# Inverting the recurrence's triangular blocks by 32x32 tiles of TensorE, with a last step that joins pairs

## The reference, cut to what matters

```python
def _rwkv7_step(S, inp):
    r, w, k, v, kk, b = inp
    sa = jnp.einsum('bhvk,bhk->bhv', S, kk)
    S = S * w[:, :, None, :] - sa[..., None] * b[:, :, None, :] + v[..., None] * k[:, :, None, :]
    return S, jnp.einsum('bhvk,bhk->bhv', S, r)
S_f, y_f = lax.scan(_rwkv7_step, S0_f, (r, decay[:, :, 0], kd[:, :, 0], v, kk, bd[:, :, 0]))
S_b, y_b = lax.scan(_rwkv7_step, S0_b, (r, decay[:, :, 1], kd[:, :, 1], v, kk, bd[:, :, 1]), reverse=True)
```

## Time and profile before

| | us |
|---|---|
| median of 3 runs | 4876.69 (4873.02 to 4878.9) |
| the profiled execution, first to last instruction | 4866.1 |
| TensorE matmuls busy | 4241.5 (87%) |
| DVE busy | 2749.5 (57%) |
| ACT busy | 1537.1 (32%) |
| POOL busy | 1475.8 (30%) |

### The profile page before, as it was taken

The page is one execution under the profiler, slowest core; times in us unless marked ns, Lnnn a source line. Parts: engine busy times, 40 slices in busy tenths (PEclk is TensorE's granted clock), DMA queues, the critical chain, the costliest instruction groups (busy, mean ns, idle before and its releaser), DMA issues. The chain is left out here.

```text
span 4866.1 us, 103654 instructions
## 1 busy us (share of the span) xinstructions
PE 4241.5 (87%) x43026; PEld 3280.6 (67%) x43026; DVE 2749.5 (57%) x4666; ACT 1537.1 (32%) x2721; POOL 1475.8 (30%) x1090
## 2 busy tenths in 40 slices
PE   6999889877998799989986998689788988978898
PEld 4887688854667587778884666578545677854566
DVE  3465444455666447544445665665575656557565
ACT  1332222223552123222222553210155421015542
POOL 2232233302013323233331111565232135523213
PEclk8999999988999899989998999789899999989999
DMA  6455532342135445642324133533403253340325
GB/s 194 146 186 189 145 78 59 81 159 83 42 83 178 148 153 198 197 122 71 78 59 148 45 92 112 172 99 106 149 7 81 67 183 124 104 142 17 81 53 181
DMA packets 517941, 561.41 MB, mean 115 GB/s; under 512 B 112732, under 2 KB 412284, under 8 KB 515380
## 3 DMA queue, kind: packets, MB, share of 16 engines
q1 hardware_dynamic: 389876, 475.93, 31.6%
q10 hardware_dynamic: 127616, 78.95, 5.6%
HBM read 366.75 MB, written 192.23 MB: 115 GB/s over the span
## 5 line engine op out<-in xcount | busy, mean ns | idle before, releaser
L1096 PE MATMUL pr_acc<-hH,pr_wh 128*128 128x512 f32 (+1 forms) x1288 | 482.4, 375 | 0.0
L1097 PE MATMUL pr_acc<-hL,pr_wh 128*128 128x512 f32 (+1 forms) x1288 | 466.0, 362 | 0.0
L1098 PE MATMUL pr_acc<-hH,pr_wl 128*128 128x512 f32 (+1 forms) x1288 | 465.6, 361 | 0.0
L2586 ACT ACTIVATE an_p<-an_p,an_stat 128x1280 f32<-128x1280 f32 (+5 forms) x372 | 339.7, 914 | 162.8 <-DVE an_stat L2664 157.2
L2033 POOL TENSOR_TENSOR rk_ml<-rk_lmask,rk_g 128x384 f32<-128x384 f32 x240 | 232.1, 999 | 464.1 <-DVE rk_g L1963 464.1
L2526 PE MATMUL an_t<-ident,an_p 128*128 128x128 f32 x2152 | 319.5, 283 | 40.3 <-ACT an_pT L2593 27.8
L2619 POOL TENSOR_TENSOR an_kl<-an_k,an_kh 128x1280 fp32r<-128x1280 f32 (+3 forms) x36 | 78.5, 2179 | 898.5 <-DVE an_qh L2644 898.5
L2526 PEld LDWEIGHTS an_t<-ident,an_p 128*128 128x128 f32 x2152 | 236.7, 142 | 163.9 <-issue 68.0
L2660 DVE CUSTOM_DVE_ANT_0 an_p<-an_s,an_mask 128x256 f32<-128x256 f32 (+8 forms) x308 | 274.9, 892 | 101.7 <-PE an_s L2509 68.4
L1971 DVE TENSOR_TENSOR rk_tu<-rk_tu,rk_ps 128x512 f32<-128x512 f32 x300 | 190.3, 634 | 237.0 <-PE rk_ps L1796 237.0
L1465 POOL TENSOR_TENSOR sp_sl<-sp_w,sp_sh 128x512 fp32r<-128x512 f32 x172 | 246.0, 1437 | 196.8 <-DVE sp_sh L1540 178.4
(11 more groups left out here) (382 smaller groups left out, 10181.1 us busy)
## 6 DMA issues: line engine op xcount, KB each, us to landing
CHK<-ri_out SPq DMA_DIRECT2D x24, 1920.0 KB, 8.1
rk_in<-CHK SPq DMA_DIRECT2D x120, 384.0 KB, 5.9
pr_w<-in_w_in ACTq DMA_DIRECT2D x58, 512.0 KB, 4.1
UT<-pr_out SPq DMA_DIRECT2D x45, 640.0 KB, 4.6
sp_w<-in_w_in ACTq DMA_DIRECT2D x50, 512.0 KB, 5.2
U<-sp_c SPq DMA_DIRECT2D x100, 256.0 KB, 2.0
mod_w<-in_w_mod SPq DMA_DIRECT2D x16, 1024.0 KB, 8.0
mo_w<-in_w_out SPq DMA_DIRECT2D x16, 1024.0 KB, 9.6
```

The costliest lines, as they stand in the source:

```text
L1096: nc.tensor.matmul(out, wh[:, u, k, 0:m], hi, start=(k == 0), stop=False)
L1097: nc.tensor.matmul(out, wh[:, u, k, 0:m], lo, start=False, stop=False)
L1098: ins = nc.tensor.matmul(out, wl[:, u, k, 0:m], hi, start=False, stop=(k == KT - 1))
L2586: nc.scalar.activation(row, row, ACT.Exp, bias=stat[:, n % NPM, j, 1:2], scale=heads[groups[n][0]].scale, accum_out=total[:, n % 4, j:j + ...
```

## The change

The five levels of 64x64 become four levels on diagonal pieces of 32x32 (`QB`) and a last step of another kind.

- Levels 1 to 4: each product is 32x32 with 32 columns, and four of them (one per 32 partitions, `quarter`) take the place of two. `TU`, `Ws` and `ML` hold 32 columns instead of 64, so the evictions by ACT and DVE and the masks by POOL are half as wide, and POOL makes `ML` for both heads in one instruction.
- Last step: `level_w` multiplies the piece that joins the two halves of a chunk with one half's inverse (two products of 32x32 per problem in the place of two of 64x64). `join` computes the correction and, with a product with minus the identity, moves the other half's inverse beside it. DVE writes both, negated, to a new tile `LU`. `join` of group 1 uses the banks of `state`, and waits for its evictions; group 0 of `outputs` waits for group 1 of the join's eviction instead.
- `solve` makes 32 of a chunk's 64 rows from `LU` (64 rows of the array) and 32 from `TU` (32 rows), two products in the place of one.
- `grams` writes the first piece of `G` as two halves of 32 columns (near, the diagonal quarters, and far, the ones between), with eight products each, and the rest by one product of 64 and one of 128 columns.
- One more constant, `eye`, is loaded, and the masks change with it.

```diff
                     for d in range(2):
-                        for j, arr in enumerate((A_BH, A_KH)):
+                        for far in range(2):
+                            for i in range(4):
+                                for h in range(2):
+                                    o = bank[h][quarter[i], d * 256 + far * QB:d * 256 + (far + 1) * QB]
+                                    nc.tensor.matmul(o, D[half[h], u, g, d, A_BH, quarter[i]], D[half[h], u, g, d, A_KT, quarter[i ^ far]],
+                                                     start=True, stop=True)
+                        for arr, a0, n, at0 in ((A_BH, A_RT, 1, CH), (A_KH, A_KT, 2, P)):
                             for c in range(2):
                                 for h in range(2):
-                                    rows, tok = half[h], half[c]
-                                    o = bank[h][half[c], d * 256 + j * P:d * 256 + (j + 1) * P]
-                                    ins = nc.tensor.matmul(o, D[rows, u, g, d, arr, tok], D[rows, u, g, d, A_KT:A_RT + 1, tok],
+                                    o = bank[h][half[c], d * 256 + at0:d * 256 + at0 + n * CH]
+                                    ins = nc.tensor.matmul(o, D[half[h], u, g, d, arr, half[c]], D[half[h], u, g, d, a0:a0 + n, half[c]],
                                                            start=True, stop=True)
...
                     for q in range(4):
-                        for c in range(2):
-                            ins = nc.tensor.matmul(wbank(u, g)[half[c], q * CH:(q + 1) * CH], TU[half[c], u, g, q, 1, :],
-                                                   pair[half[c], :], start=True, stop=True)
+                        for i in quarter:
+                            ins = nc.tensor.matmul(wbank(u, g)[i, q * QB:(q + 1) * QB], TU[i, u, g, q, 1, :], eye[i, 0, :],
+                                                   start=True, stop=True)
...
                         d, h = q // 2, q % 2
-                        for c in range(2):
-                            ins = nc.tensor.matmul(wbank(u, k)[half[c], q * CH:(q + 1) * CH], ML[half[c], u, g, d, h, lv, :],
-                                                   TU[half[c], u, g, q, 0, :], start=True, stop=True)
+                        if lv < NLEV - 1:
+                            for i in quarter:
+                                ins = nc.tensor.matmul(wbank(u, k)[i, q * QB:(q + 1) * QB], ML[i, u, g, d, h, lv, :],
+                                                       TU[i, u, g, q, 0, :], start=True, stop=True)
+                        else:
+                            for c in range(2):
+                                i, far = quarter[2 * c + d], quarter[2 * c + 1 - d]
+                                ins = nc.tensor.matmul(wbank(u, k)[far, h * QB:(h + 1) * QB], G[i, u, g, d, h, 0, QB:CH],
+                                                       TU[i, u, g, q, 0, :], start=True, stop=True)
...
-                    o = dbank(n).rearrange("p (q a k) -> p q a k", q=4, a=2)
+                    o = dbank(n)[:, 0:8 * QB].rearrange("p (q a k) -> p q a k", q=4, a=2)
                     for q in range(4):
-                        if lv < NLEV - 1:
+                        for i in quarter:
+                            nc.tensor.matmul(o[i, q, 0, :], TU[i, u, g, q, 1, :], Ws[i, g, q, :], start=True, stop=True)
+                        for i in quarter:
+                            ins = nc.tensor.matmul(o[i, q, 1, :], Ws[i, g, q, :], TU[i, u, g, q, 1, :], start=True, stop=True)
+                    ins.then_inc(pd.sem, 1)
+
+                def join(b, u, g):
+
+                    n = ND - NP + g
+                    pe.wait_ge(aw.sem, aw.nth(NW * b + NW - 2 * NP + g + 1))
+                    if g == 0:
+                        pe.wait_ge(dl.sem, dl.nth(ND * b + n))
+                    elif g == 1:
+                        pe.wait_ge(dh.sem, dh.nth(2 * b))
+                        pe.wait_ge(dy.sem, dy.nth(2 * b))
+                    else:
+                        pe.wait_ge(dl.sem, dl.nth(ND * b + n - 1))
+                    o = join_at(g)
+                    for h in range(2):
+                        for d in range(2):
                             for c in range(2):
-                                nc.tensor.matmul(o[half[c], q, 0, :], TU[half[c], u, g, q, 1, :], Ws[half[c], g, q, :],
-                                                 start=True, stop=True)
-                        for c in range(2):
-                            ins = nc.tensor.matmul(o[half[c], q, 1, :], Ws[half[c], g, q, :], TU[half[c], u, g, q, 1, :],
-                                                   start=True, stop=True)
+                                i, far = quarter[2 * c + d], quarter[2 * c + 1 - d]
+                                nc.tensor.matmul(o[i, d, h, :], Ws[far, g, h, :], TU[far, u, g, 2 * d + h, 1, :], start=True, stop=True)
+                                ins = nc.tensor.matmul(o[far, d, h, :], eye[far, 1, :], TU[far, u, g, 2 * d + h, 1, :],
+                                                       start=True, stop=True)
                     ins.then_inc(pd.sem, 1)
...
                     for q in range(4):
+                        d, h = q // 2, q % 2
                         for c in range(2):
-                            ins = nc.tensor.matmul(wbank(u, k)[half[c], q * P:(q + 1) * P], TU[half[c], u, g, q, 1, :],
-                                                   X[half[c], g, q, :], start=True, stop=True)
+                            near, far = quarter[2 * c + d], quarter[2 * c + 1 - d]
+                            nc.tensor.matmul(wbank(u, k)[far, q * P:(q + 1) * P], LU[half[c], g, d, h, :], X[half[c], g, q, :],
+                                             start=True, stop=True)
+                            ins = nc.tensor.matmul(wbank(u, k)[near, q * P:(q + 1) * P], TU[near, u, g, q, 1, :], X[near, g, q, :],
+                                                   start=True, stop=True)
                     ins.then_inc(pw.sem, 1)
...
-                        pe.wait_ge(dh.sem, dh.nth(2 * b))
-                        pe.wait_ge(dy.sem, dy.nth(2 * b))
+                        pe.wait_ge(dl.sem, dl.nth(ND * b + ND - 1))
                         pe.wait_ge(dbk.sem, dbk.nth(NP * b + NP))
...
-                    both = slice(0, 2) if lv < NLEV - 1 else slice(1, 2)
-                    o = TU[:, u, g, :, both, :]
-                    nc.vector.tensor_tensor(o, o, dbank(n).rearrange("p (q a k) -> p q a k", q=4, a=2)[:, :, both, :],
-                                            ALU.subtract).then_inc(dl.sem, 1)
+                    if lv < NLEV - 1:
+                        o = TU[:, u, g, :, :, :].rearrange("p q a k -> p (q a k)")
+                        nc.vector.tensor_tensor(o, o, dbank(n)[:, 0:8 * QB], ALU.subtract).then_inc(dl.sem, 1)
+                    else:
+                        nc.vector.tensor_scalar(LU[:, g], join_at(g), -1.0, None, ALU.mult).then_inc(dl.sem, 1)
...
                         for d in range(2):
-                            for h in range(2):
-                                ins = nc.gpsimd.tensor_tensor(ML[:, u, g, d, h, :, :], lm[:, d, :, :],
-                                                              G[:, u, g, d, h, 0:1, :].to_broadcast([P, NLEV, CH]), ALU.mult)
+                            ins = nc.gpsimd.tensor_tensor(ML[:, u, g, d], lm[:, d, :, :].unsqueeze(1).to_broadcast([P, 2, NLEV - 1, QB]),
+                                                          G[:, u, g, d, :, 0:1, 0:QB].to_broadcast([P, 2, NLEV - 1, QB]), ALU.mult)
```

More of the change, by code:

```diff
@@ L1597 @@
 NLEV = 6
+QB = CH // 2
 def rwkv_core(core):
@@ L1642, in rwkv_core @@
         half = [slice(0, CH), slice(CH, P)]
+        quarter = [slice(i * QB, (i + 1) * QB) for i in range(P // QB)]
         def wbank(u, k):
@@ L1648, in dbank, with join_at @@
             return bank[4 + (n + 1) % 2]
+        def join_at(g):
+            i = 6 if g == 1 else 4
+            return banks[:, i * 512:(i + 2) * 512].rearrange("p (d k) -> p d k", d=2)[:, :, 0:2 * QB].rearrange("p d (h k) -> p d h k", h=2)
         def qbank(g, c):
@@ L1882, in block_of @@
                         level_w(b, u, lv, 1)
-                        level_d(b, u, lv, 0)
-                        level_w(b, u, lv, 2)
-                        level_d(b, u, lv, 1)
-                        level_d(b, u, lv, 2)
+                        if lv < NLEV - 1:
+                            level_d(b, u, lv, 0)
+                            level_w(b, u, lv, 2)
+                            level_d(b, u, lv, 1)
+                            level_d(b, u, lv, 2)
+                        else:
+                            join(b, u, 0)
+                            level_w(b, u, lv, 2)
+                            join(b, u, 1)
+                            join(b, u, 2)
                         first = isinstance(b, int) and b == 0
@@ L3586, in constants @@
     f["mask_gram"] = np.zeros((2, P, 4 * CH))
```

(12 more changed lines are left out.)

22 lines of the change are left out of this document (14 added, 8 removed).

## The result

The changed kernel takes 5787.56 us (median of 4 runs, 5780.1 to 5793.56), the kernel before 4874.85 (4 runs, 4869.65 to 4878.9). The ratio is 1.187, 95% interval 1.185 to 1.189. The sign was forecast, the size was not: 5350 us was predicted, and 5787.56 lies above the range. About half of the +913 us has a cause that the prediction had priced at 1 us per block.

What follows compares the result with a forecast made beforehand. TensorE, fed by instruction pages, was taken as the bound: 67.0 (pages) + 1.5 (head) + 1.0 (solve) = 69.5 us per block against 45.9, times 20 is +472 us, about 5350 us, range 5210 to 5500.

Steps and rivals of the forecast that it cites:

- the solve: Solve's alternating 64-row and 32-row products: 1.0 us per block (0 to 6) beyond the time of their instruction pages.
- 100 ns or more: Sign in the solve: this start-to-start spacing would indicate the switches rival; 27 ns would mean no switch cost.
- would only show at head and solve: Half granted clock: outputs at 29 ns a pair, no more than a page costs; belongs to the range's upper end.
- switches: Rival: all 48 solve shape switches per block paid, 0.15 us each, +5 instead of +1 after absorption; 5430 us, chance 0.15.
- Absorption by neighbours: Outputs next to the solve, at 14.6 ns, would absorb up to 1.9 us of switch cost in each page.
- The pages: TensorE's instructions arrive in pages of some 252 records, one at a time, 3.77 us each; 17.8 pages, 67.0 us per block.
- The levels of before run just at the speed at which instructions arrive: Kernel before's levels: 14.6 ns per record (29 ns a pair) needed, against 15.0 ns per record from pages.
- State: State step of each block: 48 products, counted as unchanged.
- rivals of hidden pages: Two rivals where page fetches cost nothing: no gain, issue floor 14.6 ns, 4905 us; or faster, 4675 us; chance 0.07 each.
- Faster: Rival: pages hidden and quarter tiles at 7.3 ns; -10.1 us per block, 4675 us, chance 0.07.
- floor of 14.6 ns: Rival of hidden pages without gain: issue floors at 14.6 ns a pair; +1.4 us per block, 4905 us, chance 0.07.
- Head, moved waits, DVE, ACT, POOL: Block head 1.5 us (0 to 3) above its pages; moved waits nothing; savings on DVE, ACT, POOL worth nothing, longer idle.

Runs made afterwards that it cites:

- b1: Kernel before, each solve product split into one of 64 rows and one of 32 rows, issued by turns: 5289.93 us, ratio 1.085.
- b2: Kernel before, solve products split as in b1, but in each group all 64-row products first, then the 32-row ones: 4898.04 us, ratio 1.005.
- b7: Kernel before, solve's chunk 0 product left 64x64, chunk 1's split into two of 64x32, all with 64 rows: 5009.21 us, ratio 1.028.
- b6: Kernel before, split and alternated as in b1, but both products use 64 rows, so only their place changes: 4897.61 us, ratio 1.004.
- a1: Kernel after, solve reordered: in each group the eight 64-row products first, then the eight 32-row ones: 5370.18 us, ratio 1.102 to the kernel before.
- b5: Kernel before, level products, evictions and subtractions cut to 32 of 64 columns, as many instructions, half the levels' work left out: 4897.19 us, ratio 1.005.
- a3: a1 with four quarter products of levels 1 to 4 made one of 128 stationary, 32 moving columns, operands incorrect: 5753.75 us, 1.180 to kernel before.

## Why the prediction was wrong

**The step that failed is the solve.** The prediction took 1.0 us (0 to 6) above the solve's own pages, "near the lower end since both shapes use the same columns of output". The solve measured 25.9 us; its 192 instructions are 0.76 page, 2.9 us, so the excess is 23.0. The prediction's own sign for it came true: "100 ns or more" from start to start in the solve "says the rival", and it is 280 ns. The term contains three errors.

1. Only the gap between shapes was priced. At the head of a block a switch falls once in many records; in the solve it falls at every product, so each product is alone on the array as well. b1 at full clock: 0.33 us per product, where the larger product of the earlier trace rows takes 54 ns x 2 = 0.11 and the same products grouped take 0.08 (b2, 3.7 us for 48). By the starts of the single records, 0.13 of the 0.33 lie between the product's own two records and 0.20 are the way to the next shape, more than the 0.18 that the head's rows had given at most. 48 x 0.33 = 15.8 us, 12.9 above the pages.
2. TensorE's clock fell. At the lower of its two clocks (granted 0.50 between 1001.30 and 1019.30 us) a product takes 0.56, 0.21 and 0.35 of it. By the clock at each record's start, 24.3 of the solve's 25.9 us ran there. That is the other 10.1. The prediction had said of a lower clock that it "would only show at head and solve", and had put no price on that.
3. The argument that the same columns of output might let the shapes stand side by side had no row behind it. In b1 the shapes differ in rows alone and pay; b7 shows that with equal rows they pay too.

The rival "switches" named the mechanism (each of the 48 is paid) and had 0.15 of the chance; its price was too small as well. The Trainium skill ("TensorEngine Tiling (Array Packing)", section "Key Properties") states that a change of tiling mode drains the engine. The runs agree (b1 against b2, and b6, where only the tile changes and nothing is paid), and a1 shows it in the changed kernel. With the page's rule alone the sign and the place were to be had, the size not: it gives no figure.

**Absorption by neighbours** ("up to 1.9 in each page"): wrong. The outputs became 1.2 us longer instead (9.1 us; 8.1 in a1, where the solve's products are grouped). The absorption was worked out with outputs at 14.6 ns per record. Behind the solve of the kernel after, 241 of their 288 records ran at the lower clock, 27 ns apart, so instructions that had come in the meantime could not be used faster than new ones arrive.

**The pages** were right as a mechanism and close in size. The kernel after without its alternation (a1) takes 71.8 us per block where 67.0 for pages and 1.5 for the head were forecast, and 5370 us where 5350 were; 177 packets where 175 to 180 were; stops mostly every 126 to 128 records, 150.7 us of "issue" in the levels where there had been 2.5. The levels with join, 1296 record pairs in 35.3 us, ran at 3.4 us per 252 instructions, and the grams, 2.3 pages in 10.3 us, at 4.5; 3.77 is a fair mean, but all of it was read where the DMA engines were idle; with them busy a page took 5.15 us, which the sum had no term for. (4464 records by 252 are also 17.7 pages and not 17.8, 66.8 us.) The Trainium skill ("Runtime: NRT & Kernel Launch", "Instruction fetch mechanics") has blocks of 256 instructions and calls the crossing mostly hidden. The trace agrees on the size, about 252 records of TensorE to a packet, and not on the hiding: 150.7 us of stops.

**"The levels of before run just at the speed at which instructions arrive"** was half the truth. b5 shows that the array with weights of 64 columns sets nearly the same pace, 28 ns, and that at half the clock it alone sets 53.

**State, +2.5 us**, was held equal. In the kernel after (and in a1) it runs largely at the lower clock: the granted clock is 0.63 and 0.70 over the recurrence, beside 0.96. 82 of its 96 records per block ran there, and in rows of eight they start 53 ns apart, where the full clock gives 29: that is 2.0 of the 2.5. The levels lose nothing that way: at the lower clock records of 32x32 still start 13 ns apart in a burst, and the supply gives a pair every 30. No run holds the clock up, so how much of a1's excess over 69.5 is the clock's stays open. What makes it fall is shown for the solve in the kernel before (b1 against b2); for the levels it is open, since a1 and a3 have it low in very different streams.

**The rivals of hidden pages** fell. "Faster" had the array nearly right: quarter tiles reach 8.8 ns in the burst shown, and 8 in others, where it said 7.3. It had the supply wrong. A floor of 14.6 ns does not exist.

**Head, moved waits, DVE, ACT, POOL**: the head fell by 0.9 instead of rising by at most 3; the waits are nowhere to be seen. The other engines wait longer, as forecast; DVE's subtractions from 566 to 1494 us, beside the 115.5 us of the earlier trace rows:

```profile
L2020 DVE TENSOR_TENSOR rk_tu<-rk_tu,rk_ps 128x256 f32<-128x256 f32 x120 | 50.5, 421 | 261.2 <-PE rk_ps L1815 261.2
```

## What to carry to other kernels

Count TensorE's instructions before its columns: in this long unrolled program of small fp32 products each instruction costs about 15 ns of supply (a record pair 30), so a change that halves the work of a product and doubles their number loses, and joining two products that share weights wins. Put products of one tile shape together: by turns, each product cost 0.33 us where 0.08 was its share when grouped, and 0.56 once the clock had fallen. A price read where something happens once is no price for where it happens at every instruction: ask what overlap it undoes, and work it out at both levels of the clock.

## What the runs showed of the hardware

- A change of tile shape empties the array in either dimension: tiles 64x32 with 32x32 (b1, 0.33 us a product), 64x64 with 64x32 (b7, 0.34 to 0.36 a turn). Products of one shape at changing places do not (b6, 4897.61 us against b2's 4898.04).
- The time of a record on one tile follows the larger of the weights' columns and the moving columns. At full clock, weights' columns first: 128 and 32, 0.113 us (a3); 64 and 128, 54 ns on two tiles, 109 per tile; 64 and 32, 28 ns on two tiles, 56 per tile (b5); 32 and 32, 8.8 ns on four tiles, 35 per tile (after). The number of rows does not show: the grams' 64x32 tiles with 32 moving columns start some 5 ns apart on eight tiles, about 40 per tile (after). At the lower clock the same records take 0.21 us (a3) and 53 ns on two tiles (b5).
- Records on different tiles start as close as 8.8 ns on four tiles and some 5 on eight. The Trainium skill ("TensorE: Matmul & The Clock Gate", section "Wait — 56ns, not 53.3ns?") has a floor of about 25 ns from start to start for small products. From record to record these rows are below it; from record to record on the same tile (35 ns and more) they are not.
- A busy TensorE does not keep its clock: in a3 matmuls were busy for 572.20 of 600 us, weight loads for 529.05, at a granted clock of 0.64. Alternating shapes bring it down: in b1 62 of the solve's 96 records per block ran at the lower clock, in b2, grouped, none.
- Pages come later when other transfers run. In the kernel after: 3.86 us (median of 141) with the DMA engines under 10% busy, 5.15 (median of 17) with them over 30%. In a1: 3.84 (137) and 4.81 (16); in the kernel before 3.89 (8) and 5.49 (4). No run varied the transfers alone, so that they are the cause is not shown.
